# Two transformer blocks on one core: the second feed-forward's up groups 1 to 3 by Strassen's method, with seven quarter products for each pair of weight tiles

## The reference

```
x  = x + g1 * (concat([ret, att]) @ w_out)
h2 = modulate(rmsnorm(x, norm2_g), sh2, sc2)
x  = x + g2 * (square(relu(h2 @ w_ff1)) @ w_ff2)       # 1024 -> 4096 -> 1024
return rmsnorm(x, final_norm_g)
```

## Time and profile before

| | |
|---|---|
| time, median of 3 runs | 1664.36 us (1664.3 to 1664.38) |
| span of the profiled execution, first to last instruction | 1662.5 us |
| PE busy | 1633.7 us (98%), 12906 matmuls |
| DVE, ACT, POOL busy | 1059.4, 732.1, 98.8 us |
| granted TensorE clock, mean | 0.998 of full speed (2.4 GHz) |

### The profile page before, as it was taken

How to read it: one execution, slowest core, us unless ns; L and a number is a source line. 1 busy time by engine, 2 the same in 40 slices (tenths; PEclk the granted TensorE clock), 3 DMA queues, 4 the chain that set the end, 5 groups by cost and what they waited for, 6 DMA issues and landing times. The chain is left out here.

```text
span 1662.5 us, 30282 instructions
## 1 busy us (share of the span) xinstructions
PE 1633.7 (98%) x12906; PEld 1292.8 (78%) x12906; DVE 1059.4 (64%) x1508; ACT 732.1 (44%) x1105; POOL 98.8 (6%) x123
## 2 busy tenths in 40 slices
...
GB/s 229 85 51 75 83 117 42 41 42 98 36 171 183 127 164 136 156 162 218 192 216 112 86 92 77 114 89 26 20 2 89 86 105 101 90 101 101 101 90 51
DMA packets 51318, 172.81 MB, mean 104 GB/s; under 512 B 6129, under 2 KB 9329, under 8 KB 50417
## 3 DMA queue, kind: packets, MB, share of 16 engines
...
## 5 line engine op out<-in xcount | busy, mean ns | idle before, releaser
L376 PE MATMUL pair<-h_hi,w_hi 128*128 128x512 f32 x1008 | 402.2, 399 | 1.5 <-DVE w_lo L422 1.0
L378 PE MATMUL pair<-h_hi,w_lo 128*128 128x512 f32 x1008 | 393.0, 390 | 0.0
L377 PE MATMUL pair<-h_lo,w_hi 128*128 128x512 f32 x1008 | 392.9, 390 | 0.0
L422 DVE TENSOR_TENSOR w_lo<-w_raw,w_hi 128x1024 fp32r<-128x1024 f32 (+1 forms) x224 | 265.2, 1188 | 147.7 <-ACT w_hi L401 147.5
L401 ACT CAST w_hi<-w_raw 128x1024 fp32r<-128x1024 f32 (+1 forms) x224 | 220.9, 992 | 229.0 <-PE pair L378 212.1
L376 PEld LDWEIGHTS pair<-h_hi,w_hi 128*128 128x128 f32 x1008 | 189.3, 188 | 55.6 <-issue 16.4
L377 PEld LDWEIGHTS pair<-h_lo,w_hi 128*128 128x128 f32 x1008 | 189.5, 188 | 39.9 <-issue 2.8
L378 PEld LDWEIGHTS pair<-h_hi,w_lo 128*128 128x128 f32 x1008 | 189.3, 188 | 40.2
L376 PE MATMUL pair<-ff_f_hi,w_hi 128*128 128x512 f32 (+1 forms) x536 | 204.3, 381 | 0.6 <-DVE w_lo L422 0.6
L378 PE MATMUL pair<-ff_f_hi,w_lo 128*128 128x512 f32 (+1 forms) x536 | 203.6, 380 | 0.0
L377 PE MATMUL pair<-ff_f_lo,w_hi 128*128 128x512 f32 (+1 forms) x536 | 203.6, 380 | 0.0
...
## 6 DMA issues: line engine op xcount, KB each, us to landing
w_raw<-in_w_ff SPq DMA_DIRECT2D x128, 512.0 KB, 3.3
mod_w<-in_w_mod POOLq DMA_DIRECT2D x48, 512.0 KB, 3.7
w_raw<-in_w_in SPq DMA_DIRECT2D x22, 512.0 KB, 3.4
w_raw<-in_w_gate SPq DMA_DIRECT2D x16, 512.0 KB, 3.3
w_raw<-in_w_out SPq DMA_DIRECT2D x16, 512.0 KB, 3.3
w_raw<-in_w_rwkv SPq DMA_DIRECT2D x15, 512.0 KB, 3.3
w_raw<-in_w_da SPq DMA_DIRECT2D x12, 512.0 KB, 4.6
w_raw<-in_w_ple_gate SPq DMA_DIRECT2D x8, 512.0 KB, 3.3
```

The lines of the kernel that those rows point to most:

```text
L376: nc.tensor.matmul(out, w_hi, x_hi, start=(k == 0), stop=False)
L377: nc.tensor.matmul(out, w_hi, x_lo, start=False, stop=False)
L378: last = nc.tensor.matmul(out, w_lo, x_hi, start=False, stop=(k == kt - 1))
L422: nc.vector.tensor_tensor(lo[:, s % SPLIT_SLOTS, 0:cols], pr.raw[:, w % RAW_SLOTS, 0:cols], hi[:, s % SPLIT_SLOTS, 0:cols].bitcast(F32), A ...
```

## The change

The up tiles of groups 1 to 3 (24 tiles) are taken in 12 pairs. A pair computes 256 output rows for 512 tokens with a contraction of 1024. Each of the three is cut in two, and the 2x2 by 2x2 product is done with seven quarter products in place of eight (Winograd's form of Strassen's method). A quarter product, a **unit** here, has 4 steps of the contraction and 256 tokens, so 12 matmuls of 256 columns. The units stand in this order (weight quarter, moving quarter, bank):

The core of the diff:

```diff
+UNITS_AHEAD = 5
...
     def stream(self, sp, until):
...
             if old >= 0 and TILES[old][3]:
-                sp.wait_ge(self.lo_made, self.split_no[old])
+                sp.wait_ge(self.lo_made, self.raw_free(old))
...
+    def before(self, pe, Q, i):
+        bank = self.UNITS[i][2]
+        if bank == "w1":
+            pe.wait_ge(self.copied, Q + 1)
+        elif Q and bank in ("w0", "x1", "y0", "z0"):
+            pe.wait_ge(self.joined, 4 * (Q - 1) + {"w0": 2, "x1": 1, "y0": 3, "z0": 4}[bank])
+        if Q == 0 and self.UNITS[i][1] in self.turned_ready:
+            pe.wait_ge(*self.turned_ready[self.UNITS[i][1]])
+
+    def act(self, act, Q, i, bank, done):
+        if i == self.FIRST:
+            if Q % 4:
+                self.positives(act, Q - 1)
+            if Q:
+                act.wait_ge(self.joined, 4 * (Q - 1) + 1)
+            act.wait_ge(self.pr.job_done, done)
+            self.pr.nc.scalar.copy(self.copy, bank).then_inc(self.copied, 1)
+        if i in (4, 5) and Q % 4:
+            self.high(act, Q - 1, i - 4)
+
+    def positives(self, act, Q):
+        act.wait_ge(self.joined, 4 * Q + 4)
+        for t in range(2):
+            part = self.parts(Q)[:, t, :]
+            self.pr.nc.scalar.activation(part, part, ACT.Relu).then_inc(self.positive, 1)
+
+    def high(self, act, Q, t):
+        ff, g = self.ff, Q // 4 + 1
+        act.wait_ge(self.squared, 2 * Q + 1 + t)
...
+        self.pr.nc.scalar.copy(ff.f_hi[:, g % 2, 2 * (Q % 4) + t, :], self.parts(Q)[:, t, :]).then_inc(ff.hi, 1)
+
+    def dve(self, dve, Q, i, bank, done):
+        nc, ff = self.pr.nc, self.ff
+        if i in (5, 6) and Q % 4:
+            self.low(dve, Q - 1, i - 5)
+        dve.wait_ge(self.pr.job_done, done)
...
+    def weights(self, pool, Q):
...
+        pool.wait_ge(*pr.landed(w))
+        pool.wait_ge(*pr.landed(w + 1))
+        split("s1")
+        nc.gpsimd.tensor_tensor(s1, a21, a22, ALU.add).then_inc(self.summed, 1)
+        pool.wait_ge(self.summed, 4 * Q + 1)
+        split("s2")
+        nc.gpsimd.tensor_tensor(s2, s1, a11, ALU.subtract).then_inc(self.summed, 1)
+        nc.gpsimd.tensor_tensor(a21, a11, a21, ALU.subtract).then_inc(self.summed, 1)
+        pool.wait_ge(self.summed, 4 * Q + 2)
+        split("s4")
+        nc.gpsimd.tensor_tensor(s4, a12, s2, ALU.subtract).then_inc(self.summed, 1)
...
+    def pool(self, pool):
+        self.ff.pool_turned(pool)
+        for at in range(0, len(self.pairs), 4):
+            self.weights(pool, at)
+            self.weights(pool, at + 1)
+            for q in range(4):
+                if q < 2:
+                    self.weights(pool, at + q + 2)
+                self.squares(pool, at + q)
...
+    TURNED = {8: (0, 1), 9: (2,), 10: (3,)}
...
+    def pool_turned(self, pool):
...
+        pool.wait_ge(self.y_made, KT)
+        pool.wait_ge(self.pr.job_done, self.first_job_done + 2 * self.RAW - 1)
+        nc.gpsimd.tensor_tensor(t[:, 0, :, :], y[:, 0:h, second], y[:, 0:h, first], ALU.subtract).then_inc(self.turned_raw, 1)
```

More of the change, by code:

```diff
@@ L325, in gemm_block @@
     assert [g for batch in batches for g in batch] == list(range(len(order)))
-    def weight(g):
-        stage, n = order[g]
-        return stage.jobs[n].weight
+    job_of = [stage.jobs[n] for stage, n in order]
+    turns = [g for g, job in enumerate(job_of) if job.bank is None]
     def bank(g):
-        return pr.bank[(first_bank + g) % BANKS]
+        return job_of[g].bank if job_of[g].bank is not None else pr.bank[(first_bank + turns.index(g)) % BANKS]
     def due(split, g):
-        if split >= tiles or split > weight(g) - first_tile + (AHEAD if g >= len(first_ahead) else first_ahead[g]):
+        if split >= splits:
             return False
-        s = pr.split_no[first_tile + split] - 1
-        return s < SPLIT_SLOTS or pr.last_job[pr.split_slot[s - SPLIT_SLOTS]] <= first + g
+        key = pr.seq[first_split + split]
+        ahead = UNITS_AHEAD if key in pr.units else AHEAD if g >= len(first_ahead) else first_ahead[g]
+        if split > pr.split_no[job_of[g].key] - 1 - first_split + ahead:
+            return False
+        return pr.slot_free(key) <= first + g
     with nc.Block() as block:
@@ L366, in _ @@
                     stage, n = order[g]
-                    if k == 0 and weight(g) not in [weight(f) for f in range(g)]:
-                        pe.wait_ge(pr.lo_made, pr.split_no[weight(g)])
+                    job = stage.jobs[n]
+                    if k == 0 and job.key not in [job_of[f].key for f in range(g)]:
+                        pe.wait_ge(pr.lo_made, pr.split_no[job.key])
                     stage.ready(pe, n, k)
-                    job = stage.jobs[n]
-                    slot = (pr.split_no[job.weight] - 1) % SPLIT_SLOTS
+                    slot, col = pr.slot(job.key)
                     tile = stage.tile(k)
-                    w_hi, w_lo = hi[:, slot, tile * P:(tile + 1) * P], lo[:, slot, tile * P:(tile + 1) * P]
+                    cols = slice(col + tile * P, col + (tile + 1) * P)
+                    w_hi, w_lo = hi[:, slot, cols], lo[:, slot, cols]
                     x_hi, x_lo = job.moving[tile]
@@ L2823, in __init__ @@
         order = self.order = [(kind, g, j, half) for i, (kind, g) in enumerate(ff_order()) for j in range(8)
-                              for half in ((0, 1) if i == 0 and j < self.halved else (None,))]
+                              for half in ((0, 1) if i == 0 and j < self.halved else (None,))
+                              if not (self.paired and kind == "up" and g)]
+        if self.paired:
+            for g in range(1, FF_GROUPS):
+                at = min(n for n, (kind, gg, _, _) in enumerate(order) if kind == "down" and gg == g - 1)
+                order[at:at] = [("pair", g, q, i) for q in range(KT // 2) for i in range(len(self.paired.UNITS))]
         if self.halved:
@@ L2862, in act @@
         nc = self.pr.nc
-        kind, g, j, _ = self.order[n]
+        kind, g, j, half = self.order[n]
         if n == 0:
@@ L2870, in act @@
             self.square(act, self.ups[n], g, j)
+        elif kind == "pair":
+            self.paired.act(act, 4 * (g - 1) + j, half, bank, done)
+        elif self.paired and g < FF_GROUPS - 1 and j < 2:
+            if j == 0:
+                self.paired.positives(act, 4 * g + 3)
+            for t in range(2 * j):
+                self.paired.high(act, 4 * g + 3, t)
         elif g == FF_GROUPS - 1 and self.halved:
```

257 lines of the change are left out of this document (210 added, 47 removed).

## The result

| | before | after |
|---|---|---|
| time, median | 1664.33 us (1663.62 to 1664.38, 4 runs) | 1674.95 us (1674.19 to 1675.48, 4 runs) |
| ratio | | 1.0065, 95% interval 1.005 to 1.008 |
| span of the profiled execution | 1662.5 us | 1673.4 us |

The account below looks back on a forecast made before the run. PE was taken to bound the kernel. Group 1's +16.7 and 2 x 0.8 for groups 2 and 3 made +18.3 us, so 1664.4 + 18.3 = 1682.7, say 1682, with a range of 1661 to 1695.

Parts of the forecast that it names:

- +0.8: Groups 2 and 3: the first down job begins 44.3 us after the group's start, against 43.5 before, for each group.
- my own signs of being wrong: Low parts at 0.7 with pairs at 10.1, no U5 wait, POOL at 1.3, or D0 earlier than 43.5 us.
- PE's own share: Matmuls of the pairs: 10.08 us a pair in place of 10.88, twelve pairs saving at most 9.6 us.
- Exclusion of two-SBUF-input instructions of DVE and POOL: In the pairs, low parts and POOL's work exclude each other: 12.7 us of exclusive time in 10.08; joins are untouched.
- The loop: From low part of s1 to the next pair's: 12.3 us taken, laid out as 12.05, between 9.3 and 13.1.
- Copy behind LAST and the relus: At each loop's end: LAST, ACT's two relus and the copy follow, and PE's fourth unit waits for that copy.
- Group 1, +16.7: Group 1 begins late: pair 0 ends 13.4 us later than PE alone would give, and (c) adds 3.3.
- pair 0's 13.4: Group 1's first pair ends at 1369.4, where PE alone would give 1355.95.
- (c): Group 1: s1 of pair 0 is split 3.3 us later against this pair 0 than in the other groups, +3.3.
- Part (a): End of group 0: low parts of t1 to t4 take DVE 5.7 us, alone making unit 4 about 5.5 late.
- rival 4: POOL never lets DVE in, loops of 14.6 and 1697 us, or waits drop the clock to 1.2 GHz; chance 0.10.
- Clearing the semaphores, 0: After the barrier, on POOL alone: taken as 0, under 1 us either way.

Follow-up runs that it names:

- e11: e9 with GpSimd's four weight sums a pair replaced by memsets, so the sums are left out: 1654.41 us, 0.9938 of the kernel before.
- e2: The changed kernel with GpSimd's weight sums, moving sums and squares replaced by memsets, output not the model's: 1669.97 us, 1.0036 of the kernel before.
- e1: The changed kernel with ScalarE's copy of bank w0 put before the two relus of the pair before: 1672.47 us, 1.0049 of the kernel before.
- e3: The changed kernel with the pairs' squares made by ScalarE behind its relus, not by GpSimd: 1675.86 us, 1.0069 of the kernel before.
- e5: The changed kernel with the moving differences' high and low parts placed later and GpSimd's four moving sums held back: 1676.74 us, 1.0075 of the kernel before.
- e9: e8 with the turned low parts moved behind the relus, between a relu and its low part: 1665.55 us, 1.0007 of the kernel before.
- e8: The changed kernel with the copy first, squares on ScalarE and moving differences on VectorE: 1667.78 us, 1.0022 of the kernel before.

## Why the prediction was right, and where its sizes were off

The direction, the mechanism and the places were right: 1682 was forecast with a range of 1661 to 1695, 1675 measured, 7 us less. All of the slowing came at group 0's end and in group 1; for groups 2 and 3 even the sign was wrong (+0.8 each forecast, -0.95 measured), and of my own signs of being wrong one came: D0 less than 43.5 us after T, 42.57, with loops under 12. Step by step:

- **PE's own share, -9.6**: shown by e11, -9.7 by spans, groups from 43.52 to 40.3.
- **Exclusion of two-SBUF-input instructions of DVE and POOL**: shown by e2 and e11. It is not the whole of the loss: in the changed kernel memsets give back 5.0 us, and the rest lies in the order of the queues and the length of POOL's chain. Low parts "near 1.2" measured 1.12 from `w_raw` and 0.87 to 1.01 from the sums, and the two of `f_lo`, which I had counted among nine, were not held at all (0.68); POOL's sums "1.6 to 1.8" measured 1.44 to 1.71, joins 0.68 to 0.69.
- **The loop, 12.3**: the step that was mis-sized in groups 2 and 3. It ran as laid out, through POOL's squares. These are its six instructions from pair 2 to pair 3 of group 2:

```profile
1468.07 1.58 POOL L2975 TENSOR_TENSOR norm_sq<-w_raw 128x512 f32<-128x512 f32 x1 [2.14 <-DVE w_lo L466]
1469.73 1.61 POOL L2978 TENSOR_TENSOR norm_sq<-norm_sq,w_raw 128x512 f32<-128x512 f32 x1
1471.31 1.74 POOL L2979 TENSOR_TENSOR w_raw<-w_raw 128x512 f32<-128x512 f32 x1
1473.01 1.75 POOL L2982 TENSOR_TENSOR ff_w_sum<-w_raw,norm_sq 128x512 f32<-128x512 f32 x1
1474.72 2.93 POOL L2988 TENSOR_TENSOR ff_sq<-ff_sq 128x512 f32<-128x512 f32 x2
```

  From low part to low part of s1 it is 0.17 to POOL's start, 9.58 for the six, 1.97 for ACT's two casts and the low part: 11.72, and the copies are 11.72 apart. I had 1.9 for the last piece and 10.05 for POOL: a DVE instruction in between costs POOL 0.28 to 0.45 (sums of 1.58 to 1.75 against 1.3), where I gave it 0.55. The first loop was shorter still, 11.46. The two loops are 1.4 under my 24.6, and s1 of pair 1 was made at T+10.8 where I had 11.1; together they turn +0.8 a group into -0.95, 3.5 us in two groups. That 12.3 was picked above my own layout of 12.05 made it worse. The Trainium skill ("SBUF — State Buffer", Who interferes with whom) has the shared pair held for the whole instruction. This trace has less for a waiting POOL instruction: 0.28 to 0.45 beside a low part of 0.69, and 1689, which I had by that rule, would have been further off still.
- **Copy behind LAST and the relus**: right in the changed kernel. But it is not the only link: e1 showed the split of D0 next, which I had put down as costing nothing, and e3 a second ring of nearly the same length through ACT and DVE alone.
- **Group 1, +16.7**: 12.3 measured. The sum left out a term of its own: pair 0's 13.4 and the 3.3 of (c) come on top of the +0.8 that it gives the other groups, which makes 17.5. U5: 3.2 against 2.67. U6: 3.5 against 2.27. Relu of U7: 1360 against 1357.9, copy 1363.5 against 1360.8, fourth unit 1363.6 against 1361.2. The moving sums take 2.4 us unblocked, as I had it (2.40 and 2.41 in e5), and the third ended at 1331.6, where I had 1331.8. Part (a), the turned low parts ahead of the relus, is shown by e9 against e8: moving them behind gave 2.4 us in group 1, where I had 5.5 for them alone.
- **The clock**: I put a fall to 1.2 GHz into rival 4, as having no case in the rows. It happened and took 3.4 us of PE's time, but with waits for the copy behind both stretches. The first took nothing from the kernel; how much of the second is in the 12.3 is open, by the 0.46 us above not much. So the clock is no second error that hides the first: the waits were mis-sized, 16.7 against 12.3.
- **Clearing the semaphores, 0**: only 0.39 us of the difference lies ahead of U3, all causes together.
